# A depthwise convolution that adds up its 31 taps in a PSUM bank instead of SBUF

## The reference

```python
h = rmsnorm_2(x, norm1_g) * (1.0 + sc1) + sh1
z = h @ w_in
q_lat, kv_lat, k_rope, conv_in, gate_logits = jnp.split(z, SPLIT_POINTS, axis=-1)
q = (rmsnorm_2(q_lat, q_norm_g) @ w_uq)          # 8 heads; then rotary, attention
kv = (rmsnorm_2(kv_lat, kv_norm_g) @ w_ukv)
...
glu_a, glu_b = jnp.split(conv_in, 2, axis=-1)
u = glu_a * jax.nn.sigmoid(glu_b)                # 512 channels
u = causal_depthwise_conv(u, conv_w, conv_b)     # 31 taps per channel
u = jax.nn.silu(layernorm(u, conv_ln_g, conv_ln_b))
y = (g_attn * y_attn + g_conv * (u @ w_conv_out)) @ w_out
```

## Time and profile before

| | |
|---|---|
| three runs, median (lowest to highest) | 1979.2 us (1975.19 to 1979.4) |
| the profiled execution | 1975.65 us, span 1973.8 us |
| mean granted TensorE clock, as a share of full speed | 0.928 |
| TensorE busy | 1728.5 us, 88% |
| VectorE busy | 1257.2 us, 64% |
| ScalarE busy | 756.8 us, 38% |
| GpSimd busy | 323.0 us, 16% |

### The profile page before, as it was taken

The page is one execution under the profiler, slowest core; times in us unless marked ns, Lnnn a source line. Parts: engine busy times, 40 slices in busy tenths (PEclk is TensorE's granted clock), DMA queues, the critical chain, the costliest instruction groups (busy, mean ns, idle before and its releaser), DMA issues. The chain is left out here.

```text
span 1973.8 us, 19274 instructions
## 1 busy us (share of the span) xinstructions
PE 1728.5 (88%) x7948; PEld 1339.4 (68%) x7948; DVE 1257.2 (64%) x1545; ACT 756.8 (38%) x938; POOL 323.0 (16%) x188
## 2 busy tenths in 40 slices
PE   4979787889899987999999969989778986999985
PEld 3858676777688864878887837767433764777764
DVE  4858556783333337643454467989776645898986
ACT  4233333233412234321232224231456225666654
POOL 1000001113300002000000014423000003544440
PEclk7989888999999998999999979989899996999998
DMA  6324212333222232444434402212100204989993
GB/s 247 116 85 157 60 38 83 119 122 108 84 87 105 86 128 85 150 151 170 164 131 152 170 22 91 86 64 86 64 0 0 86 5 172 389 335 344 346 344 135
DMA packets 59638, 264.93 MB, mean 134 GB/s; under 512 B 21648, under 2 KB 22160, under 8 KB 33056
## 3 DMA queue, kind: packets, MB, share of 16 engines
q1 hardware_dynamic: 34896, 159.56, 22.7%
q0 software_dynamic: 15184, 99.90, 13.4%
q10 hardware_dynamic: 9472, 4.26, 0.8%
HBM read 240.26 MB, written 23.44 MB: 134 GB/s over the span
## 5 line engine op out<-in xcount | busy, mean ns | idle before, releaser
L363 PE MATMUL bank<-h_high,wsplit 128*128 128x512 f32 x992 | 323.5, 405 | 26.9 <-POOL wsplit L1420 8.5
L1420 DVE TENSOR_TENSOR wsplit<-ring,wsplit 128x2048 fp32r<-128x2048 f32 x77 | 176.4, 2291 | 199.0 <-ACT wsplit L862 198.9
L862 ACT ACTIVATE wsplit<-ring 128x2048 fp32r<-128x2048 f32 x98 | 186.9, 1907 | 227.5 <-PE bank L363 205.5
L363 PEld LDWEIGHTS bank<-h_high,wsplit 128*128 128x128 f32 x992 | 190.4, 192 | 81.1 <-POOL wsplit L1420 9.4
L363 PE MATMUL bank<-xn_high,wsplit 128*128 128x512 f32 (+1 forms) x832 | 221.5, 354 | 25.5 <-DVE wal_low L1453 18.5
L363 PE MATMUL bank<-h_low,wsplit 128*128 128x512 f32 x496 | 199.4, 402 | 0.0
L363 PEld LDWEIGHTS bank<-xn_high,wsplit 128*128 128x128 f32 x832 | 149.2, 195 | 47.8 <-issue 19.9
L363 PE MATMUL bank<-f_high,wsplit 128*128 128x512 f32 x512 | 167.1, 407 | 4.4 <-DVE f_low L1961 4.4
L363 PE MATMUL bank<-xn_low,wsplit 128*128 128x512 f32 (+1 forms) x416 | 145.9, 351 | 0.0
L2001 DVE SCALAR_TENSOR_TENSOR conv<-conv_in,vecs,conv 128x512 f32<-128x512 f32 x120 | 140.3, 1169 | 4.3
L1420 POOL TENSOR_TENSOR wsplit<-ring,wsplit 128x2048 fp32r<-128x2048 f32 x21 | 98.8, 4706 | 171.8 <-ACT wsplit L862 171.8
(11 more groups left out here) (470 smaller groups left out, 3368.4 us busy)
## 6 DMA issues: line engine op xcount, KB each, us to landing
ring<-in_W SPq DMA_DIRECT2D x122, 1024.0 KB, 4.9
weights_out<-prep SPq DMA_DIRECT2D x8, 864.0 KB, 5.6
prep<-weights_out_early POOLq DMA_DIRECT2D x8, 576.0 KB, 3.1
xslot<-zeros SPq DMA_DIRECT2D x7, 516.0 KB, 5.0
block<-xslot SPq DMA_DIRECT2D x7, 516.0 KB, 11.9
yslot<-block_out SPq DMA_DIRECT2D x7, 512.0 KB, 8.8
prep<-turns_early POOLq DMA_DIRECT2D x8, 288.0 KB, 2.4
x_in<-in_xT SPq DMA_DIRECT2D x4, 528.0 KB, 6.8
```

The costliest lines, as they stand in the source:

```text
L363: return g.matmul(o, l, r, start=first, stop=last_, skip_group_check=True)
L862: g.activation(wst[:, side(n), 0, :], ringt[:, n % RING, :], ACT.Copy).then_inc(*a.sig(("high", n)))
L1420: g.tensor_tensor(wst[:, side(n), 1, :], ringt[:, n % RING, :], hi, SUB).then_inc(*t.sig(("low", n), ("released", n)))
```

## The change

The 31 operations of a block of channels add up in a PSUM bank (`grown`): the first writes it, the next 29 read and write it, and the last tap reads it and writes `conv` in SBUF. The first operation of a block now waits for VectorE's operation before it, since the bank may still be being read. TensorE's program takes the bank out of rotation after the tiles of `lat` 0 and gives it back after the v tiles; VectorE waits once, before its first use, until ScalarE has read what the bank held before (a tile of `cin`). The next tile of TensorE in that bank, the mean over channels, waits for the last tap.

```diff
--- before.py
+++ after.py
@@ -174,6 +174,7 @@
              "slots_cleared", "rows_scattered", "y_stored", "out_stored")]
         values = {}
         counted = []
+        lent = {}
 
         def at(*name):
             if not counted:
@@ -652,6 +653,8 @@
                 linear("cin", i, hb, each="h2_split")
             for i in range(3):
                 linear("lat", i, hb)
+                if i == 0:
+                    lent["conv"] = banks.take("conv")[1]
             linear("ga", 0, hb)
             sqs = [acc[:, 0, :], acc[:, 1, :], nrm[:, 0, :], nrm[:, 1, :], nrm[:, 2, :]]
             for name, lo, n in (("q_ms", 0, 3), ("kv_ms", 3, 2)):
@@ -698,6 +701,7 @@
                     t = three(b, kvh[:, k, c], kvl[:, k, c], wh[:, k, 512:1024], wl[:, k, 512:1024], k == 0, k == 1)
                 t.then_inc(*p.sig(("v2", m), ("used", nkv)))
                 banks.close("v2", m)
+            banks.close("conv")
             b = fresh("conv_mean")
             p.wait_ge(*at("convolved"))
             for c in range(4):
@@ -1992,14 +1996,19 @@
             def convolve(c):
                 cw = vec("conv_w_2").rearrange("p (c k) -> p c k", k=31)
                 v.wait_ge(*at("conv_input", c))
+                grown = banks.at("conv")
+                if c == 0:
+                    v.wait_ge(*at("free", *lent["conv"]))
                 for k in range(31):
                     i = CU[:, c, k:k + 512]
                     if k == 0:
-                        g.tensor_scalar(CO[:, c, :], i, cw[:, c, 0:1], vec("conv_b_2")[:, c:c + 1], MUL, ADD).then_inc(*v.sig())
+                        v.wait_ge(*v.own())
+                        g.tensor_scalar(grown, i, cw[:, c, 0:1], vec("conv_b_2")[:, c:c + 1], MUL, ADD).then_inc(*v.sig())
                     else:
                         v.wait_ge(*v.own())
-                        g.scalar_tensor_tensor(out=CO[:, c, :], in0=i, scalar=cw[:, c, k:k + 1], in1=CO[:, c, :], op0=MUL, op1=ADD).then_inc(
-                            *v.sig(("convolved",)))
+                        o = CO[:, c, :] if k == 30 else grown
+                        g.scalar_tensor_tensor(out=o, in0=i, scalar=cw[:, c, k:k + 1], in1=grown, op0=MUL, op1=ADD).then_inc(
+                            *v.sig(("convolved",), ("free", "conv")))
 
             def conv_product(j):
                 v.wait_ge(*at("cin_out", j))
```

## The result

| | median (lowest to highest) | ratio to the kernel before, 95% interval |
|---|---|---|
| before, 5 runs | 1975.19 us (1974.48 to 1979.4) | |
| changed, 5 runs | 1956.27 us (1945.49 to 1957.63) | 0.9883 (0.9854 to 0.9911) |
| changed, again, 5 runs on another occasion | 1957.24 us (1952.25 to 1957.71) | 0.9897 (0.9879 to 0.9914) |

On the second occasion the kernel before had a median of 1977.83 us in 17 runs. So by the medians the change saves 18.9 us on the first occasion and 20.6 us on the second, 1.0 to 1.2% by the ratios. The forecast was 1955.

What follows compares the result with a forecast made beforehand. TensorE, busy 88%, was taken to bound the kernel, with late convolution taps on VectorE behind its waits. Taking 22.8 us off 1975.65 or 1979.2 gave 1952.9 or 1956.4, stated as 1955 us, range 1948 to 1961.

Steps and rivals of the forecast that it cites:

- What bounds the kernel: TensorE, busy 88% of the span; VectorE time counts only where TensorE waits, with stalls of 16.3, 8.2 and 0.8 us.
- the contention: VectorE's convolution taps beside GpSimd's operations: with one input in a bank, the whole 50.1 us of long taps goes.
- The price of a tap: VectorE's taps on the bank cost as in SBUF, 0.79 us from start to start; bounds 0.56 and 1.30 us.
- read and written in turns: Rival at VectorE's taps: a bank takes two turns per column, 1.30 us a tap, 1992 to 1996 us; chance 0.06.
- The first operation of a block: Writing a bank and waiting for the tap before costs at most 0.3 us each, 1.2 us in all, in slack.
- The first half: Blocks 0 and 1, before q's reciprocal: of 20 us or more saved, 4.4 us pass on, limited by ScalarE's root.
- The second half: Blocks 2 and 3: TensorE's work becomes later than the last tap by 4.1 us; k unit begins 22.8 us earlier.
- The bank: TensorE's rotation with seven banks: two tight tiles, fifth gate and seventh k; nothing taken for both, 1 us as bound.
- the rival that the change does nothing: GpSimd still holds off taps; TensorE's 7 us bank wait comes mostly from the 8.2 us wait; 1976 to 1981; chance 0.07.
- The sum: Whole kernel: 22.8 us off 1975.65 gives 1952.9, off the median 1979.2 gives 1956.4; 1955 us given.

Runs made afterwards that it cites:

- the pair of runs above: Changed kernel with every tap's second input in SBUF and output in the bank, 1984.29 us; and its mirror, second input in the bank and output in SBUF, 1956.96 us.
- the experiment with four more: Changed kernel with the first operation of blocks 2 and 3 issued three times in place of once: 1955.57 us, ratio 0.9875.
- the lending alone: Changed kernel with the bank still taken out of TensorE's rotation, but all four convolution blocks adding up in SBUF: 1979.26 us, ratio 1.0013.

## Why the prediction was right

*What bounds the kernel* and *the contention*: as forecast. All 50 us of long taps went, and the pair of runs above shows that it was by the second input. The nearest row that the forecast leaned on, L1707 in the earlier trace rows, has just this kind of inputs.

*The price of a tap*: 756 ns against 752, 0.79 us from start to start, as taken. Writing to a bank costs 8 ns (760 against 752 with both inputs in SBUF, 756 against 748 with the second one in the bank), reading one saves 4. The surcharge that the Trainium skill (VectorE: DVE Perf Modes, the section on the TRN2 errata) sets on a PSUM source, 65 ns a tap as estimated from its cycle counts, is not there. The bank is not read and written in turns: 116 taps do both at 756 ns.

*The first operation of a block* takes 0.81 us, 0.27 more, close to the upper bound of 0.3 that was given; in blocks 2 and 3 the experiment with four more shows that it lay in slack, and in blocks 0 and 1 it came ahead of VectorE's 16.6 us without work.

*The first half* passed on 4.4 us, from 81.77 to 77.37 us after the first product, with VectorE idle for 16.6 us and TensorE for 4.83 (4.6 forecast).

*The second half*: the last tap ends 3.7 us before ScalarE is free for the split that needs it (4.1 forecast), the 16.3 us wait is gone, GpSimd's copy holds VectorE's split for 1.1 us (1.4 forecast), and the k unit starts 23.1 us earlier (22.8 forecast).

*The bank*: no wait, as forecast for the changed kernel. In the rival that the change does nothing, its price was set at "nearly all of it taken from the 8.2 us": the lending alone costs 2.3 us of the stretch, because the late tile also holds up ScalarE's root, a path that the forecast did not have.

*The sum* hit the measured median by 1.3 us, and that closeness is partly luck. The 22.8 us were taken off 1975.65 and 1979.2, and 1955 was chosen between the results, 1952.9 and 1956.4. With two more runs the median of the kernel before is 1975.19, and 1975.19 - 22.8 = 1952.4. Between the medians lie 18.9 and 20.6 us, so the 22.8 us that the forecast passed on in full are confirmed to 0.3 us for the stretch and only to 2 to 4 us for the whole. The profiled execution of the changed kernel, at 1945.49, lay 2.5 us under the range; 8.7 us had been won ahead of the stretch.

## What to carry to other kernels

When VectorE and GpSimd work beside each other, look for a bimodal duration on VectorE (a median of 752 ns and a mean of 1169) and count its SBUF inputs: an accumulator that is passed from one operation to the next can live in a PSUM bank at nearly the same price (756 against 752 ns here), and the collision is gone. Before you count the gain, follow each engine's queue past the point that gets quicker, since here 50 us of VectorE's time gave 23, and which part counts was decided by ScalarE's order and TensorE's backlog. An idle time that the change opens (16.6 us here) names the next edit, and that edit may be worth little without the first (7.2 us of the stretch with it here, 1.2 without).

## What the runs showed of the hardware

- A one-input `tensor_scalar` on 128x512 fp32 takes 0.54 us from SBUF to SBUF and 0.81 us from SBUF to a PSUM bank, while a tap whose two inputs lie in SBUF takes 8 ns more when it writes a bank (760 against 752). The forecast had only bounded this, and no run shows why the two differ.
- Executions of one kernel on one core differ by up to 12 us (1945.49 to 1957.63) with the same instructions. Between the profiles of the kernel before and of the changed one, the 8.7 us ahead of the stretch go with 9.7 us less busy time of TensorE at a mean granted clock of 0.94 in place of 0.93. What makes the clock differ there stays open; no run was made for it.
